# A kernel of two model blocks on one core: other buffers for the glu and w_out weights, silu and parts earlier in the order, and twelve row buffers for the expert gathers

## The chip, the cores and the metric

One core of a Trainium2 chip. The time is that of one execution on the device, in microseconds; lower is better. A kernel's time is the median of its runs.

## The reference, cut to what matters

A first block (attention, then a Fourier mixer, 256 tokens of width 2048) feeds a second one. All is float32. What the change touches lies in the second:

```python
yc = conformer_conv_group(...)        # conv, layer norm with gain and bias, then c * sigmoid(c)
z = gelu(y_ssm); ys = z * sigmoid(z @ glu_w)                    # 1024 x 1024
y = concat([rms_norm(yc, grp_norm_conv_g), rms_norm(ys, grp_norm_ssm_g)])
h = h + y @ w_out                                               # 2048 x 2048
h = h + mem_cross_attention(...)
hn = rms_norm(h, norm_ffn_g)
# peer: for each token and each of 8 heads
s1, i1 = top_k(q1 @ keys1, 16); s2, i2 = top_k(q2 @ keys2, 16)  # 128 keys a side
top_s, pos = top_k(s1[:, None] + s2[None, :], 16)               # of 256 sums
idx = i1 * 128 + i2 at pos;  g = softmax(top_s)
act = gelu(hn . u[idx]);  h += sum(g * act * v[idx])            # 128 rows of u and of v a token
```

## The kernel before, in words

Every engine has a program written out by hand in its own order: SP issues the weight loads, TensorE (pe_) multiplies, VectorE (v_) and ScalarE (a_) prepare operands and take results out, GpSimd (g_) issues the gathers. Programs wait on named moments; what stands behind a wait on the same engine waits with it.

**Memory.** The ring has eight units of 8 KB per partition, numbered 0 to 7. A load takes the next unit or units in a cycle over `c.units` of them, from `c.unit_next` (sp_slot, L262), and waits until the load that held them is used. In the split products units 6 and 7 hold the parts of the weights. The arena (30 K floats per partition) holds activations; views of it are placed by offset in K1 = 1024 floats.

**A split product.** Weights come as chunks of 128 x 512, `i` counting them over all blocks. ScalarE rounds a chunk to a high part (L398), VectorE subtracts to get the low part (L410), TensorE makes three products of parts (L489 to L492 by columns, L452 to L454 by rows). Four chunks of parts exist, so ScalarE's cast of chunk i waits until TensorE is done with chunk i - 4. `split` (L513) sets the order on ScalarE and VectorE: the part of chunk i, then what stands in `at` for chunk j = i - 3 (the number is j within its block; the function gets the block), then the block's `out`, then an aside step; after a job's last chunk its `end`. Jobs follow each other without a break: the first chunks of the next job are made ahead of the last work of the one before.

**Mixer.** sp_mixer (L2288) loads w_in, tables for the state part (unit 5), phases 0 to 7 of the state part (units 4 and 3 in turn), then glu's weights (two blocks of 8 chunks, four loads of one unit, cycling over units 0 to 2) and w_out's (four blocks of 16 chunks, eight loads of two units over units 0 to 5). TensorE runs the convolution, the column sums for the conv's layer norm, glu by columns, then w_out by rows with two sums for each block: one over the conv half and one over the state half, as each half has its own norm, applied behind the product (`add`). On ScalarE, glu's `end` runs conv_silu (L2648: all eight silus, from `cen` to `convT`), and w_out's first chunks run high(0) to high(3) (L2656, the high parts of y with the norm's gain, four columns each; 0 and 1 are the conv half) and the squares for the two norms. On VectorE glu's `end` is `gated` (L2558, z times sigmoid), and low(0) to low(3) (L2562) make the low parts of y in w_out's first block. TensorE's chunk k needs the low part of the chunk and of y's group k // 4. The norms' row sums (pe_row_sums, L2407) come behind chunks 3 and 11 of the first block.

**Experts.** TensorE makes the queries: head 0 alone, head 1 alone, then two heads at a time (pe_queries, L3026), from eight weight loads of one unit in units 0 to 5. Behind head 0, head 1 and the pair 2, 3 come their key scores (pe_choose). v_choose (L3109) picks the indices: copies the scores to `sc`, top 16 of each side, `cand`, top 16 of those, `eq` to look the indices up. It runs for head 0 and for head 1 at once (L3185 to L3188: copy of the query, choice), and later in ten steps between scored rows. g_experts (L3284) waits for the last weight load and gathers 512 times 128 rows of 2048 floats, one for each of the 128 partitions, in a fixed order: 36 of u, then v and u in turn. Gather n uses buffer n modulo ten: the eight units of the ring and two of the arena, those that hold no query weights first, then the six others in the order in which TensorE uses their weights up. VectorE scores u rows (L3219) and adds most v rows (L3207), TensorE adds three of eight v rows (L3071).

## Time and profile before

| | us |
|---|---|
| median of 3 runs | 3579.13 (3578.89 to 3579.28) |
| the profiled execution, its own time | 3582.07 |
| its span | 3580.6 |

Busy shares of the span: TensorE 74%, VectorE 74%, GpSimd 43%, ScalarE 29%. Mean rate of the DMA engines: 272 GB/s. Mean granted TensorE clock: 0.87 (1 is 2.4 GHz). The page gives shares over the whole span; a change to one stage has to be read in that stage, from the rows further down. All times in rows are from the start of the span.

### The profile page before, as it was taken

To read this page: it belongs to the slowest core of one execution; us is meant where nothing else is said; L and a number is where in the kernel's file an instruction comes from. 1 tells how busy PE (TensorE), PEld (TensorE's weight loads), DVE (VectorE), ACT (ScalarE), POOL (GpSimd) and SP (SyncE) were. 2 spreads that over 40 slices of the span, in tenths; PEclk is the share of its full clock that TensorE was granted. 3 is DMA by queue.
4 is the path that set the end of the run, shared out by engine and by line. 5 is a ranking of instruction groups with operands and counts; after the bars stand their busy time and mean duration, and the time that the engine had idled before them with its cause. 6 is when DMAs were issued, how large, how long until landed. Compare 5 with 4: busy or idle time off the path is not lost.

```text
span 3580.6 us, 35597 instructions
## 1 busy us (share of the span) xinstructions
PE 2650.4 (74%) x13300; PEld 2047.9 (57%) x13300; DVE 2657.4 (74%) x3789; ACT 1055.2 (29%) x1961; POOL 1554.6 (43%) x1943
## 2 busy tenths in 40 slices
PE   7989999987999999799988999614444444434445
PEld 6867897555999987699676897501111111111112
DVE  8977887767566655578855555798889798888775
ACT  2255253233444444354665535000000000000000
POOL 7887777750000000000000000387877776876663
PEclk9999999998999999999998999856676676776668
DMA  9876766634376645443204544799999999999998
GB/s 371 324 257 228 244 231 218 222 131 175 106 257 231 230 143 186 178 163 130 83 26 175 188 142 159 278 415 420 422 422 422 422 422 422 405 422 421 422 421 349
DMA packets 277965, 974.07 MB, mean 272 GB/s; under 512 B 14497, under 2 KB 30497, under 8 KB 208929
## 3 DMA queue, kind: packets, MB, share of 16 engines
q0 software_dynamic: 76592, 551.58, 37.2%
q1 hardware_dynamic: 198848, 411.70, 32.9%
q10 hardware_dynamic: 2352, 8.52, 0.6%
q8 instruction: 104, 1.70, 0.2%
q14 instruction: 69, 0.56, 0.0%
HBM read 957.07 MB, written 14.68 MB: 271 GB/s over the span
## 4 chain that ended last, share of the span: by engine, by line
PE 54%; DMA 19%; DVE 14%; POOL 6%; ACT 3%; issue 3%; ACTq 0%; SPq 0%; DVEq 0%; POOLq 0%
DMA ring<-in_peer_v,arena 9%; PE lin L489 7%; PE lin L491 6%; PE lin L492 6%; DMA ring<-in_peer_u,arena 5%; PE lin L452 5%; PE lin L454 5%; PE lin L453 5%; PE lin L3071 5%; POOL ring L3302 5%; PE lin L356 3%; PE lin L2374 3%; DMA arena<-in_peer_v,arena 2%; DVE mod_sums L811 2%; DVE weight_parts L410 2%
## 5 line engine op out<-in xcount | busy, mean ns | idle before, releaser
L410 DVE TENSOR_TENSOR weight_parts<-ring,weight_parts 128x512 fp32r<-128x512 f32 (+2 forms) x1010 | 687.7, 693 | 497.8 <-ACT weight_parts L398 492.1
L3071 PE MATMUL lin<-ring,diag 128*128 128x512 f32 x632 | 436.0, 854 | 619.8 <-DMA ring<-in_peer_v,arena 471.4
L398 ACT CAST weight_parts<-ring 128x512 fp32r<-128x512 f32 (+2 forms) x1010 | 610.9, 611 | 796.7 <-PE lin L492 386.5
L3071 PEld LDWEIGHTS lin<-ring,diag 128*128 128x128 f32 x632 | 168.9, 281 | 882.8 <-issue 809.9
L489 PE MATMUL lin<-parts,weight_parts 128*128 128x256 f32 x1984 | 571.0, 288 | 10.4 <-DVE weight_parts L410 10.4
L491 PE MATMUL lin<-parts,weight_parts 128*128 128x256 f32 x1984 | 564.3, 284 | 0.0
L492 PE MATMUL lin<-parts,weight_parts 128*128 128x256 f32 x1984 | 564.1, 284 | 0.0
L3219 DVE CUSTOM_DVE_ANT_0 ring<-ring,arena 128x2048 f32<-128x2048 f32 x204 | 465.5, 2290 | 128.8 <-DMA ring<-in_peer_u,arena 121.9
L2772 POOL DMA_DIRECT2D arena<-mem_keys x1 | 0.6, 575 | 1240.5 <-DVE weight_parts L410 1240.5
L3302 POOL DMA_INDIRECT ring<-in_peer_u,arena x204 | 373.7, 1832 | 338.0 <-DVE arena L3120 226.5
L452 PE MATMUL lin<-weight_parts,parts 128*128 128x512 f32 (+2 forms) x1124 | 435.2, 387 | 45.5 <-DVE weight_parts L410 21.8
L3302 POOL DMA_INDIRECT ring<-in_peer_v,arena x206 | 370.6, 1799 | 184.6 <-PE lin L3071 125.5
L453 PE MATMUL lin<-weight_parts,parts 128*128 128x512 f32 (+2 forms) x1124 | 426.3, 379 | 0.0
L454 PE MATMUL lin<-weight_parts,parts 128*128 128x512 f32 (+2 forms) x1124 | 426.3, 379 | 0.0
L489 PEld LDWEIGHTS lin<-parts,weight_parts 128*128 128x128 f32 x1984 | 383.5, 193 | 16.4 <-DVE weight_parts L410 12.4
L491 PEld LDWEIGHTS lin<-parts,weight_parts 128*128 128x128 f32 x1984 | 383.8, 193 | 0.4
L492 PEld LDWEIGHTS lin<-parts,weight_parts 128*128 128x128 f32 x1984 | 383.5, 193 | 0.0
L3207 DVE SCALAR_TENSOR_TENSOR arena<-ring,arena 128x2048 f32<-128x2048 f32 x127 | 298.5, 2350 | 40.0 <-DMA ring<-in_peer_v,arena 38.1
L452 PEld LDWEIGHTS lin<-weight_parts,parts 128*128 128x128 f32 x1124 | 213.7, 190 | 100.9 <-DVE weight_parts L410 33.4
L454 PEld LDWEIGHTS lin<-weight_parts,parts 128*128 128x128 f32 x1124 | 213.6, 190 | 39.3
L453 PEld LDWEIGHTS lin<-weight_parts,parts 128*128 128x128 f32 x1124 | 214.0, 190 | 37.4 <-issue 1.0
L811 DVE SCALAR_TENSOR_TENSOR mod_sums<-ring,silu_c,mod_sums 128x512 f32<-128x512 f32 x240 | 187.5, 781 | 5.2 <-DMA ring<-in_ada_w 0.8
(298 smaller groups left out, 3780.6 us busy)
## 6 DMA issues: line engine op xcount, KB each, us to landing
ring<-in_ada_w SPq DMA_DIRECT2D x96, 1024.0 KB, 8.3
ring<-in_w_in_fourier SPq DMA_DIRECT2D x64, 1024.0 KB, 8.2
ring<-in_w_kv_mem SPq DMA_DIRECT2D x32, 1024.0 KB, 7.6
ring<-in_w_in_attn SPq DMA_DIRECT2D x32, 1024.0 KB, 5.3
ring<-in_w_out_fourier SPq DMA_DIRECT2D x16, 2048.0 KB, 8.0
ring<-in_w_in SPq DMA_DIRECT2D x24, 1024.0 KB, 5.1
ring<-in_w_out_attn SPq DMA_DIRECT2D x8, 2048.0 KB, 8.6
ring<-in_w_out SPq DMA_DIRECT2D x8, 2048.0 KB, 8.2
```

The costliest lines, as they stand in the source:

```text
L398: c.nc.scalar.copy(c.w_parts[:, q, 0, 0:w], c.slot(load, L.kc, w)[:, k % L.kc, :]).then_inc(c.a_high.after(("high", L.name, i)), 1)
L410: c.nc.vector.tensor_tensor(c.w_parts[:, q, 1, 0:w], c.slot(load, L.kc, w)[:, k % L.kc, :], c.w_parts[:, q, 0, 0:w].bitcast(F32), ALU.subt ...
L452: c.nc.tensor.matmul(banks[t][:, 0:w], lhs(0, k, t), hi, start=(k % part == 0), stop=False)
L453: c.nc.tensor.matmul(banks[t][:, 0:w], lhs(0, k, t), lo, start=False, stop=False)
L454: mm = c.nc.tensor.matmul(banks[t][:, 0:w], lhs(1, k, t), hi, start=False, stop=(k % part == part - 1))
L489: c.nc.tensor.matmul(o, hi[:, b], rhs(0, k), start=(k == 0 and j % 2 == 0), stop=False, skip_group_check=True)
L491: c.nc.tensor.matmul(o, hi[:, b], rhs(1, k), start=False, stop=False, skip_group_check=True)
L492: mm = c.nc.tensor.matmul(o, lo[:, b], rhs(0, k), start=False, stop=(k == L.K - 1), skip_group_check=True)
L3071: mm = nc.tensor.matmul(X.sums[t][b][:, :], c.diag[:, X.diag_of(t, k), :], X.buf_of[t, 1, k][:, b * 512:(b + 1) * 512], start=(k == PE_ROW ...
L3207: nc.vector.scalar_tensor_tensor(out=X.H[:, t, :], in0=X.buf_of[t, 1, k], scalar=X.act[:, t, k:k + 1], in1=X.H[:, t, :], op0=ALU.mult, op1 ...
L3219: c.nc.vector.tensor_tensor_reduce(out=buf, in0=buf, in1=X.hn[:, t, :], scale=1.0, scalar=0.0, op0=ALU.mult, op1=ALU.add, accum_out=X.act[ ...
L3302: c.nc.gpsimd.indirect_dma_start(X.bufs[q], None, X.tables[table], bass.IndirectOffsetOnAxis(ap=X.idx[:, t, k:k + 1], axis=0)).then_inc(go ...
```

## The change

In sp_mixer glu's loads cycle over units 0 to 3, and w_out's begin at unit 4. The silus run in pairs behind chunks 3 to 6 of glu's second block, and the conv half's high and low parts behind its chunk 7, ahead of the sigmoid of that block and of `gated`. For that y's low parts are placed elsewhere (6 K1 and 19 K1). The other high and low parts and the squares for the conv norm shift by a few chunks, and the row sums of the conv norm go from chunk 3 to chunk 5. In the experts `sc`, `cand` and `eq` hold one group of heads instead of all, and two row buffers of 8 KB take the place that is left (17 and 19 K1). Head 1's query is copied by ScalarE, behind its part of the turned activations.

```diff
@@ -2261,7 +2261,13 @@
         self.stat = c.at(29 * K1, 4, SEQ)
         self.token = c.st[:, 42:54].rearrange("p (a b t) -> p a b t", a=2, b=3)
         self.L = Lin("w_out_mix", c.I["w_out_2"][0], 0, D)
-        self.R = Residual(c, self.L, "y_mix", c.at(9 * K1, KD * SEQ), c.at_r(25 * K1, KD * SEQ), c.at_r(17 * K1, KD * SEQ))
+        self.y = c.at(9 * K1, KD * SEQ)
+        self.y_hi = c.at_r(25 * K1, KD * SEQ)
+        self.y_lo = [c.at_r(6 * K1, NC * SEQ), c.at_r(19 * K1, NC * SEQ)]
+
+    def y_cols(self, a, k, t):
+        part = self.y_hi[:, k * SEQ:(k + 1) * SEQ] if a == 0 else self.y_lo[k // NC][:, k % NC * SEQ:(k % NC + 1) * SEQ]
+        return part[:, t * P:(t + 1) * P]
 
     def lo_part(self, q):
         return self.lo[q // 2][:, q % 2 * 1024:(q % 2 + 1) * 1024]
@@ -2300,8 +2306,9 @@
         yield from sp_load(c, (L.name, b, ch), L.src(b, w, ch), L.kc, w, units=1)
     for k in range(2, NC):
         yield from sp_phases(c, k)
+    c.units, c.unit_next = 4, 0
     yield from sp_weights(c, X.glu_lin)
-    c.units, c.unit_next = 2 * RING - 2, 0
+    c.units, c.unit_next = 2 * RING - 2, 4
     yield from sp_weights(c, X.L)
 
 
@@ -2400,8 +2407,8 @@
 
     yield from pe_split_cols(c, X.glu_lin, "z", X.z_cols, at={3: conv_variance})
     first = lambda f: lambda b: nothing() if b else f
-    yield from pe_split_rows(c, X.L, (X.R.name,), X.R.lhs, sums=2,
-                             at={3: first(pe_row_sums(c, "conv_rms", X.tmp)), 11: first(pe_row_sums(c, "ssm_rms", X.tmp2))})
+    yield from pe_split_rows(c, X.L, ("y_mix",), X.y_cols, sums=2,
+                             at={5: first(pe_row_sums(c, "conv_rms", X.tmp)), 11: first(pe_row_sums(c, "ssm_rms", X.tmp2))})
 
 
 def pe_row_sums(c, name, x):
@@ -2561,13 +2568,18 @@
 
     def low(q):
 
-        R, (_, g) = X.R, GROUP_NORMS[q // 2]
-        yield from v.wait_ge(("high", R.name, q))
+        g = GROUP_NORMS[q // 2][1]
+        yield from v.wait_ge(("high", "y_mix", q))
         for k in range(4 * q, 4 * q + 4):
-            s = slice(k * SEQ, (k + 1) * SEQ)
-            nc.vector.scalar_tensor_tensor(out=R.lo[:, s], in0=R.yT[:, s], scalar=c.col(g, k % NC), in1=R.hi[:, s].bitcast(F32),
-                                           op0=ALU.mult, op1=ALU.subtract).then_inc(
-                c.v_low.after(*([("low", R.name, q)] if k % 4 == 3 else [])), 1)
+            s, r = slice(k * SEQ, (k + 1) * SEQ), slice(k % NC * SEQ, (k % NC + 1) * SEQ)
+            nc.vector.scalar_tensor_tensor(out=X.y_lo[k // NC][:, r], in0=X.y[:, s], scalar=c.col(g, k % NC),
+                                           in1=X.y_hi[:, s].bitcast(F32), op0=ALU.mult, op1=ALU.subtract).then_inc(
+                c.v_low.after(*([("low", "y_mix", q)] if k % 4 == 3 else [])), 1)
+
+    def conv_low(b):
+        if b == 1:
+            yield from low(0)
+            yield from low(1)
 
     def add(b, half):
         n, w = X.L.blocks[b]
@@ -2585,9 +2597,8 @@
 
     first = lambda f: lambda b: nothing() if b else f()
     yield from v_jobs(c, [
-        Job(X.glu_lin, nothing, z_part, end=gated),
-        Job(X.L, lambda b: add(b, 1), at={0: first(lambda: low(0)), 2: first(lambda: low(1)), 5: first(lambda: low(2)),
-                                          7: first(lambda: low(3)), 9: lambda b: add(b, 0)})])
+        Job(X.glu_lin, nothing, z_part, at={NC - 1: conv_low}, end=gated),
+        Job(X.L, lambda b: add(b, 1), at={1: first(lambda: low(2)), 3: first(lambda: low(3)), 9: lambda b: add(b, 0)})])
 
 
 def v_column_rstd(c, X, name):
@@ -2645,21 +2656,24 @@
     def glu_out(b):
         yield from a_cols_act(c, X.glu_lin, lambda j: X.zs[:, j:j + 2, :], ACT.Sigmoid)(b)
 
-    def conv_silu():
-        yield from a.aside(0)
+    def conv_silu(k0):
         yield from a.wait_ge("conv_normed")
-        for k in range(NC):
+        for k in (k0, k0 + 1):
             nc.scalar.activation(X.convT[:, k, :], X.cen[:, k, :], ACT.Silu, bias=c.col("conv_ln_b", k),
                                  scale=c.col("conv_ln_g", k)).then_inc(
                 step.after(*(["conv_silu"] if k == NC - 1 else [])), 1)
 
     def high(q):
-        R, (_, g) = X.R, GROUP_NORMS[q // 2]
+        g = GROUP_NORMS[q // 2][1]
         yield from a.wait_ge("conv_silu" if q < 2 else "gated")
         for k in range(4 * q, 4 * q + 4):
             s = slice(k * SEQ, (k + 1) * SEQ)
-            nc.scalar.activation(R.hi[:, s], R.yT[:, s], ACT.Copy, scale=c.col(g, k % NC)).then_inc(
-                c.a_high.after(*([("high", R.name, q)] if k % 4 == 3 else [])), 1)
+            nc.scalar.activation(X.y_hi[:, s], X.y[:, s], ACT.Copy, scale=c.col(g, k % NC)).then_inc(
+                c.a_high.after(*([("high", "y_mix", q)] if k % 4 == 3 else [])), 1)
+
+    def conv_high():
+        yield from high(0)
+        yield from high(1)
 
     def squared(name, x, tmp, ready):
         yield from a.wait_ge(ready, ("full", ("sum", "conv_ln")))
@@ -2670,14 +2684,17 @@
         yield from a_rstd(c, name, (X.token[:, half, 1, :], X.token[:, half, 2, :]))
 
     first = lambda f: lambda b: nothing() if b else f()
+    second = lambda f: lambda b: f() if b == 1 else nothing()
     a.side, a.rate, a.owed = [a_conv_norm(c, X)], 0.5, 0
     yield from a_jobs(c, [
-        Job(X.glu_lin, glu_out, z_part, end=conv_silu),
+        Job(X.glu_lin, glu_out, z_part, at={
+            3: second(lambda: conv_silu(0)), 4: second(lambda: conv_silu(2)), 5: second(lambda: conv_silu(4)),
+            6: second(lambda: conv_silu(6)), 7: second(conv_high)}),
         Job(X.L, a_block_squares(c, X.L, X.H), at={
-            0: first(lambda: high(0)), 1: first(lambda: high(1)),
-            2: first(lambda: squared("conv_rms", X.convT, X.tmp, "conv_silu")), 4: first(lambda: high(2)), 6: first(lambda: high(3)),
+            0: first(lambda: high(2)), 2: first(lambda: high(3)),
+            3: first(lambda: squared("conv_rms", X.convT, X.tmp, "conv_silu")),
             7: first(lambda: squared("ssm_rms", X.ysT, X.tmp2, "gated")), 9: first(lambda: roots(0)), 15: first(lambda: roots(1))})])
-    c.moments[(X.R.name, "squares")] = (c.a_step.sem, c.a_step.value)
+    c.moments[("y_mix", "squares")] = (c.a_step.sem, c.a_step.value)
 
 
 def a_conv_norm(c, X):
@@ -2914,9 +2931,9 @@
         self.f_row = c.at(10 * K1, D)
         self.qT = c.at(12 * K1, E_HEADS, SEQ)
         self.keys = c.at(14 * K1, E_HEADS, E_KEYS)
-        self.sc = c.at(15 * K1, E_HEADS * 2, E_KEYS)
-        self.cand = c.at(17 * K1, E_HEADS, TOPK, TOPK)
-        self.eq = c.at(19 * K1, E_HEADS, TOPK, TOPK)
+        self.sc = c.at(15 * K1, HH * 2, E_KEYS)
+        self.cand = c.at(15 * K1 + 512, HH, TOPK, TOPK)
+        self.eq = c.at(16 * K1, HH, TOPK, TOPK)
         small = c.at(21 * K1, 16, 256)
         self.v1 = small[:, 0, :]
         self.i1 = small[:, 1, :].bitcast(U32)
@@ -2933,7 +2950,7 @@
         self.act = c.at(25 * K1 + 256, NT, E_SLOTS)
         self.idx = c.at(25 * K1 + 512, NT, E_SLOTS).bitcast(U32)
         self.bufs = [c.ring[:, i // 2, (i % 2) * D:(i % 2 + 1) * D] for i in range(2 * RING)] + [
-            c.at(26 * K1, D), c.at(28 * K1, D)]
+            c.at(17 * K1, D), c.at(19 * K1, D), c.at(26 * K1, D), c.at(28 * K1, D)]
         self.buf_of = {}
         self.tables = (c.I["peer_u_2"][0], c.I["peer_v_2"][0])
         self.sums, self.added, self.diag_holder = {}, None, {}
@@ -3117,18 +3134,18 @@
     for sd in range(2):
         key = ("key_scores", t, h0, sd)
         yield from v.wait_ge(("full", key))
-        nc.vector.tensor_copy(sc[:, hs, sd, :], c.bank[key][:, 0:n * E_KEYS].rearrange("p (a b) -> p a b", a=n)).then_inc(
+        nc.vector.tensor_copy(sc[:, 0:n, sd, :], c.bank[key][:, 0:n * E_KEYS].rearrange("p (a b) -> p a b", a=n)).then_inc(
             step.after(("free", key)), 1)
     yield True
     i1q, v1q = (x.rearrange("p (q k) -> p q k", k=TOPK) for x in (X.i1, X.v1))
-    yield from v_top16(c, lambda q: X.sc[:, 2 * h0 + q, :], lambda q: v1q[:, 2 * h0 + q, :],
+    yield from v_top16(c, lambda q: X.sc[:, q, :], lambda q: v1q[:, 2 * h0 + q, :],
                        lambda q: i1q[:, 2 * h0 + q, :], 2 * n)
     v1, i1f = halves(X.v1), halves(X.i1f)
     nc.vector.tensor_copy(X.i1f[:, ls], X.i1[:, ls]).then_inc(step.after(), 1)
-    vt(X.cand[:, hs], v1[:, hs, 0, :].unsqueeze(3).broadcast_to([P, n, TOPK, TOPK]),
+    vt(X.cand[:, 0:n], v1[:, hs, 0, :].unsqueeze(3).broadcast_to([P, n, TOPK, TOPK]),
        v1[:, hs, 1, :].unsqueeze(2).broadcast_to([P, n, TOPK, TOPK]), ALU.add).then_inc(step.after(), 1)
     tv, pv = by_head(X.top), by_head(X.pos)
-    yield from v_top16(c, lambda q: X.cand[:, h0 + q, :, :].rearrange("p a b -> p (a b)"),
+    yield from v_top16(c, lambda q: X.cand[:, q, :, :].rearrange("p a b -> p (a b)"),
                        lambda q: tv[:, h0 + q, :], lambda q: pv[:, h0 + q, :], n)
     vs(X.pi[:, ks], X.pos[:, ks], 4, None, ALU.logical_shift_right).then_inc(step.after(), 1)
     vs(X.pj[:, ks], X.pos[:, ks], 15, None, ALU.bitwise_and).then_inc(step.after(), 1)
@@ -3138,14 +3155,14 @@
     yield from v.wait_ge(step)
     iota = c.iota[:, :].unsqueeze(1).broadcast_to([P, TOPK, TOPK])
     for f, sd, e in ((X.pif, 0, X.e1), (X.pjf, 1, X.e2)):
-        for h in range(h0, h0 + n):
-            vt(X.eq[:, h], by_head(f)[:, h, :].unsqueeze(2).broadcast_to([P, TOPK, TOPK]), iota, ALU.is_equal).then_inc(
+        for h in range(n):
+            vt(X.eq[:, h], by_head(f)[:, h0 + h, :].unsqueeze(2).broadcast_to([P, TOPK, TOPK]), iota, ALU.is_equal).then_inc(
                 step.after(), 1)
         yield from v.wait_ge(step)
-        vt(X.eq[:, hs], X.eq[:, hs], i1f[:, hs, sd, :].unsqueeze(2).broadcast_to([P, n, TOPK, TOPK]), ALU.mult).then_inc(
+        vt(X.eq[:, 0:n], X.eq[:, 0:n], i1f[:, hs, sd, :].unsqueeze(2).broadcast_to([P, n, TOPK, TOPK]), ALU.mult).then_inc(
             step.after(), 1)
         yield from v.wait_ge(step)
-        nc.vector.tensor_reduce(by_head(e)[:, hs, :], X.eq[:, hs], AX_X, ALU.add).then_inc(step.after(), 1)
+        nc.vector.tensor_reduce(by_head(e)[:, hs, :], X.eq[:, 0:n], AX_X, ALU.add).then_inc(step.after(), 1)
         yield from v.wait_ge(step)
         yield True
     nc.vector.scalar_tensor_tensor(out=X.idxf[:, ks], in0=X.e1[:, ks], scalar=float(E_KEYS), in1=X.e2[:, ks],
@@ -3183,7 +3200,8 @@
         names = [("used", "ffn_g")] if t == NT - 1 else []
         vt(X.hn[:, t, :], X.hn[:, t, :], g_row, ALU.mult).then_inc(step.after(*names), 1)
     for h in range(HH):
-        yield from v_copy_out(c, ("query", h), X.qT[:, h, :], lambda: c.bank[("query", h)][:, 0:SEQ])
+        if h == 0:
+            yield from v_copy_out(c, ("query", h), X.qT[:, h, :], lambda: c.bank[("query", h)][:, 0:SEQ])
         v.side = [v_choose(c, X, 0, h, 1)]
         yield from v.aside(0)
     for n, (t, table, k) in enumerate(ORDER):
@@ -3245,6 +3263,8 @@
     yield from a_rms_rows(c, "ffn_x", lambda t: X.H[:, t, :], lambda t: X.hn[:, t, :])
     for q in range(KD // 4):
         yield from a_turn_out(c, ("ffn_x", q), lambda k: X.cols(4 * q + k), 4, NT, gain=lambda k: c.col("ffn_g", 4 * q + k))
+    for h in range(1, HH):
+        yield from a_copy_out(c, ("query", h), X.qT[:, h, :], lambda: c.bank[("query", h)][:, 0:SEQ])
     for h in range(HH):
         yield from a_choose(c, X, 0, h, 1)
     for h in range(HH, E_HEADS, HH):
```

## Rows read from the trace of the kernel before

**Rows 1.** The page's slices: rate of the DMA engines in each of 40 equal slices.

```profile
GB/s 371 324 257 228 244 231 218 222 131 175 106 257 231 230 143 186 178 163 130 83 26 175 188 142 159 278 415 420 422 422 422 422 422 422 405 422 421 422 421 349
```

**Rows 2.** Chain of waits, 1835 to 1975: start us, us, what.

```profile
1874.93 9.35 DMA ring<-in_w_out
...
1888.26 4.04 ACT arena L2652 x8
...
1892.80 1.61 ACT parts L2661 x4
1894.44 1.68 DVE parts L2568 x4
...
1903.81 4.76 PE aux L2414 x32
...
1921.79 3.47 PE aux L2414 x32
```

**Rows 3.** Timeline of ScalarE (ACT): start us, us, engine, line, op, tiles, count, idle before.

```profile
1872.07 0.62 ACT L398 CAST weight_parts<-ring 128x512 fp32r<-128x512 f32 x1 [0.82 <-PE lin L492]
...
1885.87 1.07 ACT L2160 ACTIVATE arena<-lin 128x512 f32<-128x512 f32 x2
1886.96 1.28 ACT L2652 ACT_TABLE_LOAD   x1
...
1913.62 0.62 ACT L398 CAST weight_parts<-ring 128x512 fp32r<-128x512 f32 x1 [1.58 <-PE lin L454]
```

**Rows 4.** Timeline of VectorE (DVE), same stretch.

```profile
1847.01 1.23 DVE L426 TENSOR_TENSOR parts<-arena,parts 128x1024 fp32r<-128x1024 f32 x1 [20.01 <-ACT parts L420]
...
1887.07 2.29 DVE L2560 TENSOR_TENSOR arena<-arena 128x2048 f32<-128x2048 f32 x1 [0.22 <-ACT arena L2160]
```

**Rows 5.** TensorE's timeline, then windows: busy times by engine, granted clock, DMA share, GB/s.

```profile
1896.25 0.77 PE L452 MATMUL lin<-weight_parts,parts 128*128 128x512 f32 x1 [17.02 <-DVE parts L2568]
...
1882.00:1883.50 1.50, 0.00 (x0) 0.00 (x0) 0.00 (x0) 0.00 (x0) 0.00 (x0) 0.63 1.06 392
...
1907.50:1912.00 4.50, 4.50 (x15) 3.73 (x15) 0.00 (x0) 0.57 (x1) 0.00 (x0) 0.50 1.04 381
```

**Rows 6.** Timelines at the queries: TensorE three rows, ScalarE one.

```profile
2252.48 0.80 PE L3021 MATMUL aux<-arena 64*128 64x128 f32 x4 [4.64 <-DVE arena L368]
2253.21 16.35 PE L3037 MATMUL lin<-arena,ring 128*128 128x256 f32 x64
...
2270.89 27.89 PE L3037 MATMUL lin<-arena,ring 128*128 128x256 f32 x128
...
2269.60 0.58 ACT L373 COPY arena<-lin 128x512 f32<-128x512 f32 x1 [5.67 <-PE lin L3037]
```

**Rows 7.** Timelines at the first gathers: last weight load (SP), GpSimd (POOL), all gathers' landing.

```profile
2247.88 0.37 SPq L280 DMA_DIRECT2D ring<-in_peer_w_q  x1
...
2253.97 1.02 POOL L3302 DMA_INDIRECT ring<-in_peer_u,arena  x1 [226.47 <-DVE arena L3120]
...
2299.06 1.83 POOL L3302 DMA_INDIRECT ring<-in_peer_u,arena  x1 [5.97 <-PE lin L3037]
...
DMA to landing us min/median/max: 5.6/18.7/22.2
```

**Rows 8.** Windows in the experts, columns as in rows 5.

```profile
2251.00:2257.00 6.00, 4.52 (x13) 3.58 (x14) 4.53 (x26) 0.21 (x1) 2.43 (x3) 0.50 0.44 128
2400.00:2420.00 20.00, 5.37 (x8) 2.03 (x8) 20.00 (x27) 1.48 (x2) 18.17 (x7) 0.79 0.95 383
2820.00:2840.00 20.00, 9.84 (x12) 4.03 (x13) 14.01 (x11) 0.81 (x3) 13.34 (x9) 0.59 1.02 424
3040.00:3060.00 20.00, 10.30 (x16) 3.70 (x15) 18.90 (x26) 1.69 (x2) 18.48 (x6) 0.84 0.95 381
3060.00:3080.00 20.00, 6.64 (x9) 2.63 (x9) 19.58 (x37) 0.00 (x0) 15.93 (x12) 0.59 0.97 385
```

**Rows 9.** Timeline of VectorE, the tenth gathered row.

```profile
2307.32 2.29 DVE L3219 CUSTOM_DVE_ANT_0 ring<-ring,arena 128x2048 f32<-128x2048 f32 x1 [6.45 <-DMA ring<-in_peer_u,arena]
```

## The prediction, made before the changed kernel was run

> **What bounds the kernel now.** I read four views in this order. The slices first [rows 1]: from the 27th on the DMA engines move 415 to 422 GB/s (one slice 405) until the last, of 349, so that stretch (the experts) is bound by the bytes of its 512 row gathers of 1.049 MB each, 2.485 us apiece at 422 GB/s. Before it the rate is mostly a half to a third of that, and the chain of waits runs mostly through TensorE. Only four places of the kernel can be worth anything to this change: the hand-over from the gate product (glu) to w_out, the hand-over from the queries to the gathers, and two dents in the saturated stretch.
>
> Hand-over to w_out: in the chain of waits [rows 2] TensorE's glu work ends at 1879.2, the first w_out load is issued at 1874.93 and lands 9.35 us later, and then eight silus, four high parts and four low parts follow one another before TensorE starts at 1896.25 after 17.02 us idle [rows 5]. Its granted clock was down at 0.50 (1.2 GHz) when it started, and again in 1907.5 to 1912 [rows 5].
>
> Hand-over to the gathers: TensorE is idle for 4.64 us until 2252.48, after head 1's query, waiting for VectorE's copy of it, which stands behind head 0's whole choice [rows 6]. Six of the ten row buffers hold query weights, so GpSimd issues four gathers from 2253.97 on and then one each time TensorE is done with a weight chunk (six of them, 4 to 8 us apart); the tenth goes out at 2299.06 [rows 7]. Only from there are the DMA engines full.
>
> **Part 1, glu and w_out in units of their own.** Today glu cycles through three units and w_out's first load (two units) needs one that glu's last chunk holds. With the change glu's last load takes unit 3 and w_out's first units 4 and 5, held by tables and phases that VectorE's state work has read by 1827 (it is idle for 20.01 us before 1847.01 [rows 4]). Both loads then land before 1845. That removes the wait for the DMA. On SP nothing is moved ahead of anything late: the other w_out loads follow in the same order, the second when glu's first two chunks are used (about 1863), and it is not needed before 1900.
>
> **Part 2, silu and parts inside glu's second block.** I lay out ScalarE from the casts of [rows 3]; silu's input is ready before that. Cast 14 ends at 1872.7. Table load 1.28 and two silus of 0.505: 1875.0. Cast 15 (0.6) ends at 1875.6; TensorE needs its low part at 1877.8, so glu isn't delayed: slack 1.5. Then silu pair, cast 16, silu pair, cast 17, silu pair, cast 18: 3 x (1.0 + 0.6) gives 1880.4. Two high groups of 1.7: 1883.8. The sigmoid of block 1, which stood right behind the casts, now waits for all this and needs its table again: 1.28 + 1.07, done 1886.2. VectorE: the first low group ends at 1883.8, the second at 1885.5, the gating product of 2.29 [rows 4] at 1888.5.
> So TensorE starts w_out at 1883.9 instead of 1896.25, 12.3 earlier. What is late next: w_out's fourth chunk, whose low part stands behind the gating product on VectorE: ready 1889.2. ScalarE's high(2) waits for the gating product too, and casts 20 and up are queued behind it, TensorE behind them: cast 20 at 1890.8, low parts of chunks 4 and 5 at 1891.5 and (behind low(2), 1.67) 1893.8. Chunk 5 ends at 1895.3. The sums of the conv norm, moved from behind chunk 3 to behind chunk 5, wait for a square of 1.9 that ends at 1895.5, and take 3.5 to 4.8 (4.76 for them here, 3.47 for the other norm's [rows 2]): done 1899.1 to 1900.4. The old kernel has chunk 5 and the same sums done at 1913.6 (the cast released then [rows 3]). From there both do the same work at the same pace. Gain 13.2 to 14.5; I take **13.5**. Bounds: 14.5 with the clock at 2.4 GHz in the sums; 11 if half clock lasts 4.4 us into chunks 6 and 7 as it did around 1907 to 1912, which costs 2.2. TensorE's gap shrinks from 17 to 4.7 us, but the clock fell about 3.2 us after the matmuls stopped (granted 0.63 in 1882 to 1883.5 [rows 5]), so I let it fall.
> The change makes ScalarE switch tables once more. In [rows 3] the Silu switch takes 1.28 and the first silu begins 0.02 behind it; two such switches stand in my chain. ("ScalarE: Activation LUTs" of the Trainium skill, What ACT_TABLE_LOAD costs, puts every switch at 1283 ns and a drain of about 1380 ns. The trace has the 1.28 and nothing of a drain. By the page, as an estimate, both switches together cost 2.8 more, and the gain would be about 11.)
> Memory stage: TensorE-bound, its loads follow TensorE; all of it only moves earlier. Profile rows below are given in the old kernel's times.
>
> **Part 3, head 1's query copied by ScalarE.** ScalarE is idle there; a copy of twice the size takes 0.58 [rows 6]. TensorE has the scores' input at 2248.4 and starts the next query group at 2249.1 instead of 2253.21: 4.1. The gap of 4.64 also cost clock (granted 0.50 from 2251 to 2257 [rows 8]): that group took 16.35 us and the next ones 13.9 each [rows 6]. With a gap of 0.7 there is no fall: 2.5 more. Sum **6.6**. The last chunk is then used at 2292.4. VectorE loses a copy of 0.42. GpSimd's first gather doesn't move: it waits for the last weight load, issued at 2247.88 when head 1's matmuls are done, 6.1 before that gather [rows 7].
>
> **Part 4, two more buffers.** Six gathers go out before the first wait, not four, and twelve have gone when the last chunk is used. DMA has idle time for them there. **2 x 2.485 = 4.97.** VectorE gains as much: it has scored rows 1 to 9 when row 10 lands at 2307.3, after 6.45 idle [rows 9]; now it is row 12 that lands at 2300.7, with two rows (4.6) and a choice step (1.1) less left, 12.3 in all against the DMA's 11.6.
> The dents: 383 GB/s in 2400 to 2420, 381 and 385 in 3040 to 3080 [rows 8] against 422, that is 1.85 + 1.94 + 1.75 = **5.5** us, where the buffers were all with VectorE (busy 20.0, 18.9 and 19.6 of 20). Two more rows of slack are 4.97 in each, more than either dent, so I take all back. The scratch shared by the groups costs nothing: all its users are VectorE, in the same order, and each step already waits for the last. A third buffer-related wait: a group's indices are ready by its 15th scored row, the gather that needs them is issued at the 20th or later.
>
> **Sum**: 13.5 + 6.6 + 5.0 + 5.5 = 30.6. Against the profiled execution's own 3582.07 that is 3551.5; the three runs have a median of 3579.13, 2.9 lower, so I forecast **3548.5**. Its own range is 3543 to 3553: 14.5 in the mixer on one side, with 4 for waits that fall differently; 11 and half the dents on the other.
>
> **Rivals.**
> A, chance 0.17: the dents stay (VectorE's backlog, not the number of buffers, sets them) and the query group stays slow: 13.5 + 4.1 + 5.0 = 22.6, **3556.5**. For it: VectorE is busy 20.0 of 20 in the first [rows 8]. Against: in dents of under 2 us two rows are enough.
> B, 0.09: in w_out the clock and the queue on ScalarE take back more, so that only 9 is left there: **3553**.
> C, 0.04: nothing of parts 3 and 4 reaches the end, as VectorE becomes the bound from 2300 on: 13.5, **3565.6**. Against it: further on VectorE is busy only 14.0 of 20 [rows 8].
> D, 0.03: SP's w_out load still comes late because a unit isn't free; parts 1 and 2 then give 10.5 (cast at 1884.3, start at 1885.8): **3551.5**.
> E, 0.02: deeper queue, higher rate. "DMA: Bandwidth & Descriptors" (Trainium skill, Specifications) has a fabric ceiling of 435 GB/s, which would be 3% more; as an estimate 38 us, 3511. In rows alone: 422 is moved with ten in flight, and the highest window of 20 us has 424 [rows 8], 0.5% or 6 us more, **3542**.
> F, slower, 0.03: twelve gathers in flight on one queue, two of them into memory beside the scratch that VectorE uses in each choice, lower the rate of all gathers in the 1250 us from 2300 on. Each per cent costs 12.5, so 2.5% (411 GB/s) eats the gain and 3.2% makes **3588**. For it: a gather lands up to 22.2 us after its issue as it is [rows 7], a queue already deep. Against: from the 28th slice to the last but one all but one keep 420 to 422 [rows 1], whatever the engines do.
> G, 0.02: both hand-overs give back three quarters, under 7.2 is left: **3573**.
>
> **Numbers.** 0.2% is 7.2 us, about what a measurement of this kernel can tell from no change. Faster: forecast 0.60 and A to E, 0.95; same 0.02 (G); slower 0.03 (F). The range for eight in ten, 3543 to 3560, takes in forecast, A, B and D, and the joint low bounds 11 + 8.9.
>
> **What the next profile would show.** Right: w_out's first load issued by 1830; TensorE idle under 6 us before its first w_out matmul, near 1884; head 1's copy on ScalarE, the gap before the second scores under 1 us and the query group at 13.9; six gathers before GpSimd's first wait on TensorE; slices of 421 to 423 with no dent. Wrong: glu matmuls waiting for cast 15 or 16; TensorE idle over 3 us at chunks 3 to 5; a gather rate under 418; VectorE idle for landings gone but DMA share under 1.

## The result, and the profile after

The changed kernel takes 3560.18 us (median of 6 runs, 3556.59 to 3567.35), beside 3579.2 for the kernel before in 6 runs on the same chip: a ratio of 0.9946, 95% interval 0.9936 to 0.9957, 19 us or 0.54% less. The two were run again beside the last experiments: 3557.76 (5 runs) against 3581.89 (9 runs), 0.9937, 0.9923 to 0.9951. Forecast were 3548.5, range 3543 to 3560: right in sign, 11.7 us too low, and at the very edge of the range (by the medians 0.2 us above it, by the ratio, 0.9946 x 3579.13 = 3559.8, 0.2 inside).

**How stages are compared.** The program of the first 1840 us is the same in all kernels, yet glu's first product stands anywhere between 1843.66 and 1855.62 us in the fourteen profiled executions. What follows repeats far better, so I measure from event to event in each profiled execution: glu's first product, w_out's first product, the memory stage's first transpose on TensorE, the experts' first transpose, and VectorE's addition of the last gathered row. The two profiled executions of the changed kernel differ by 0.02, 0.02, 0.00 and 0.16 us in these. Across kernels that have the same program in a stretch the scatter is larger: the four with the old mixer give 47.30 to 47.59 and 152.56 to 152.89 us up to w_out and to the memory stage, but 224.54 to 226.24 from there to the experts; the four with the old experts (before, mixer part, units, silu and parts) give 1339.23 to 1339.95. One execution's difference under 0.7 us (1.6 in the memory stage) therefore shows nothing by itself; that the new mixer costs the memory stage 1.4 us rests on five executions of 227.52 to 227.62. The last column has the median of the runs; units, silu and parts, copy, buffers and ten buffers ran once each.

| us | glu to w_out | glu to memory | memory to experts | experts to last row | time |
|---|---|---|---|---|---|
| before | 47.36 | 152.65 | 226.10 | 1339.72 | 3579.2 |
| after | 34.67 | 141.01 | 227.52 | 1327.07 | 3560.2 |
| after, once more | 34.69 | 141.03 | 227.52 | 1327.23 | 3557.8 |
| mixer part alone | 34.68 | 140.98 | 227.60 | 1339.63 | 3567.6 |
| experts part alone | 47.45 | 152.71 | 226.11 | 1327.07 | 3567.2 |
| units alone | 40.28 | 145.56 | 226.85 | 1339.23 | 3570.1 |
| silu and parts alone | 43.94 | 151.88 | 227.03 | 1339.95 | 3579.1 |
| copy alone | 47.30 | 152.56 | 224.54 | 1333.73 | 3571.9 |
| buffers alone | 47.59 | 152.89 | 226.24 | 1334.33 | 3578.3 |
| after with ten buffers | 34.68 | 141.03 | 227.60 | 1333.12 | 3565.7 |
| sums spread | 34.69 | 137.04 | 226.41 | 1328.91 | 3554.0 |
| order of reuse | 34.68 | 141.04 | 227.62 | 1318.15 | 3551.9 |
| both | 34.69 | 137.02 | 226.40 | 1319.01 | 3548.4 |
| both, first gather sooner | 34.69 | 137.02 | 226.40 | 1317.02 | 3546.2 |

By the stages the change is worth 11.64 - 1.42 + 12.65 = **22.9 us** (0.64%). That lies at the edge of the first interval and inside the second, and the 7.7 us between it and the forecast sum of 30.6 is what has to be explained. The rest of the 11.7, 4.0 us, lies in no stage that was compared: runs of one kernel lie up to 11 us apart, and the two profiled executions differ by 23.5, of which 0.62 ahead of glu.

**The hand-over to w_out.** ScalarE's timeline in the changed kernel (start us, us, engine, line, operation, tiles, count, idle before); it answers to [rows 3]:

```profile
1871.43 0.62 ACT L398 CAST weight_parts<-ring 128x512 fp32r<-128x512 f32 x1 [0.82 <-PE lin L492]
1872.07 1.28 ACT L2662 ACT_TABLE_LOAD   x1
1873.37 1.09 ACT L2662 ACTIVATE arena<-arena,colpack_sb 128x256 f32<-128x256 f32 x2
1874.37 0.60 ACT L398 CAST weight_parts<-ring 128x512 fp32r<-128x512 f32 x1
...
1879.39 3.30 ACT L2671 ACTIVATE parts<-arena,colpack_sb 128x256 fp32r<-128x256 f32 x8
1882.70 1.28 ACT L2160 ACT_TABLE_LOAD   x1
1884.00 1.09 ACT L2160 ACTIVATE arena<-lin 128x512 f32<-128x512 f32 x2
...
1887.54 1.71 ACT L2671 ACTIVATE parts<-arena,colpack_sb 128x256 fp32r<-128x256 f32 x4 [1.95 <-DVE arena L2567]
```

The silus stand between the casts and hold up nothing, the high parts follow, then the sigmoid of glu's second block. Start of w_out, from TensorE's timeline, answering to [rows 5]; then, from the chain of waits, the two blocks of row sums that answer to the L2414 rows of [rows 2]:

```profile
1882.94 0.76 PE L452 MATMUL lin<-weight_parts,parts 128*128 128x512 f32 x1 [4.35 <-DVE parts L2575]
```

```profile
1894.38 3.63 PE aux L2421 x32
...
1907.92 3.46 PE aux L2421 x32
```

TensorE starts 12.69 us sooner after glu's first product, with 4.35 idle instead of 17.02. The conv norm's sums end at 1898.0. Now windows of the same profile (us, busy time by engine, granted clock, DMA share, GB/s):

```profile
1898.00:1899.00 1.00, 1.00 (x6) 0.81 (x6) 0.00 (x0) 0.00 (x0) 0.00 (x0) 0.92 0.91 344
1899.00:1902.00 3.00, 3.00 (x9) 2.33 (x8) 0.69 (x1) 2.01 (x2) 0.00 (x0) 0.50 1.05 404
1902.00:1907.00 5.00, 5.00 (x23) 4.12 (x22) 2.27 (x8) 4.07 (x7) 0.00 (x0) 0.97 0.19 66
1913.00:1916.00 3.00, 3.00 (x9) 2.32 (x8) 0.69 (x1) 0.91 (x2) 0.00 (x0) 0.52 1.05 409
1988.00:2001.00 13.00, 9.50 (x43) 9.13 (x44) 9.12 (x17) 9.16 (x16) 0.00 (x0) 0.50 0.02 7
```

TensorE is busy throughout, yet its granted clock halves (0.50, that is 1.2 GHz) right behind each of the two blocks of sums, and again in the memory stage's first products. There the kernel before has 0.74 in the same 13 us, counted from 1.3 us ahead of the first transpose:

```profile
2000.30:2013.30 13.00, 9.54 (x55) 9.17 (x56) 9.72 (x18) 9.51 (x17) 0.00 (x0) 0.74 0.02 7
```

**The hand-over to the gathers.** TensorE, answering to [rows 6]:

```profile
2237.47 0.49 PE L3038 MATMUL aux<-arena 64*128 64x128 f32 x4 [0.46 <-ACT arena L373]
2237.89 14.08 PE L3054 MATMUL lin<-arena,ring 128*128 128x256 f32 x64
...
2253.30 27.89 PE L3054 MATMUL lin<-arena,ring 128*128 128x256 f32 x128
```

The gap of 4.64 us is 0.46, and the query group takes 14.08 instead of 16.35. GpSimd's timeline, the first, eighth, ninth and twelfth gather, answering to [rows 7]; and the time from issue to landing over all gathers:

```profile
2244.11 1.02 POOL L3322 DMA_INDIRECT ring<-in_peer_u,arena  x1 [227.46 <-DVE arena L3115]
...
2252.92 2.58 POOL L3322 DMA_INDIRECT ring<-in_peer_u,arena  x1 [0.31 <-issue]
2260.74 2.84 POOL L3322 DMA_INDIRECT ring<-in_peer_u,arena  x1 [5.24 <-PE lin L3054]
...
2281.46 3.04 POOL L3322 DMA_INDIRECT ring<-in_peer_u,arena  x1 [4.74 <-PE lin L3054]
```

```profile
DMA to landing us min/median/max: 5.8/23.8/28.0
```

Eight gathers go out before the first wait on TensorE, where I forecast six. Then the stretch in which the DMA engines are full: the page's slices, answering to [rows 1], and windows, answering to [rows 8]:

```profile
GB/s 370 310 269 227 249 230 224 228 116 178 123 231 244 239 152 169 186 150 159 43 79 163 190 143 160 312 422 422 422 422 422 422 421 422 421 422 421 422 421 331
```

```profile
2400.00:2420.00 20.00, 8.53 (x13) 3.03 (x12) 19.62 (x28) 0.00 (x0) 14.69 (x11) 0.73 1.01 421
...
3040.00:3060.00 20.00, 9.36 (x13) 3.93 (x14) 19.52 (x38) 0.00 (x0) 15.10 (x11) 0.69 1.01 419
3060.00:3080.00 20.00, 6.84 (x12) 2.46 (x10) 19.57 (x21) 2.68 (x6) 16.69 (x9) 0.83 1.01 422
```

No dent is left: 419 to 422 where 381 to 385 stood. But the last slice is lower than before, 331 against 349. I took the dents for 5.5 us of gain. That slice is the first sign that they aren't.

### The profile page after: what moved, and what is told of

Same layout as the page of the kernel before. It is cut to its first block, busy times and chain, and to the rows that moved or that the text cites. A ratio compares the mean times of both kernels' runs of the same rounds, so it can differ in the third digit from the quotient of the medians.

```text
span 3557.1 us, 35597 instructions
## 1 busy us (share of the span) xinstructions
PE 2662.4 (75%) x13300; PEld 2054.8 (58%) x13300; DVE 2654.5 (75%) x3788; ACT 1057.9 (30%) x1963; POOL 1553.6 (44%) x1943
## 4 chain that ended last, share of the span: by engine, by line
PE 53%; DMA 18%; DVE 14%; POOL 8%; issue 4%; ACT 3%; ACTq 0%; SPq 0%; DVEq 0%; POOLq 0%
PE lin L489 7%; PE lin L491 6%; PE lin L492 6%; DMA ring<-in_peer_u,arena 6%; PE lin L452 5%; PE lin L454 5%; PE lin L453 5%; DMA ring<-in_peer_v,arena 5%; POOL ring L3322 5%; DMA arena<-in_peer_v,arena 4%; PE lin L2381 3%; PE lin L3088 3%; PE lin L356 3%; POOL arena L3322 3%; DMA arena<-in_peer_u,arena 2%
## 5 line engine op out<-in xcount | busy, mean ns | idle before, releaser
L3088 PE MATMUL lin<-ring,diag 128*128 128x512 f32 x512 | 354.6, 857 | 428.3 <-DMA ring<-in_peer_v,arena 366.7
L489 PE MATMUL lin<-parts,weight_parts 128*128 128x256 f32 x1984 | 571.5, 288 | 10.5 <-DVE weight_parts L410 10.4
L3088 PEld LDWEIGHTS lin<-ring,diag 128*128 128x128 f32 x512 | 138.0, 283 | 643.1 <-issue 576.3
L3237 DVE CUSTOM_DVE_ANT_0 ring<-ring,arena 128x2048 f32<-128x2048 f32 x170 | 387.6, 2288 | 105.8 <-DMA ring<-in_peer_u,arena 99.9
L3322 POOL DMA_INDIRECT ring<-in_peer_u,arena x170 | 297.6, 1751 | 306.9 <-DVE arena L3115 227.5
L3088 PE MATMUL lin<-arena,diag 128*128 128x512 f32 x256 | 186.0, 894 | 291.7 <-DMA arena<-in_peer_v,arena 196.1
L3322 POOL DMA_INDIRECT ring<-in_peer_v,arena x170 | 314.8, 1852 | 151.9 <-PE lin L3088 102.9
L3088 PEld LDWEIGHTS lin<-arena,diag 128*128 128x128 f32 x256 | 71.6, 294 | 403.8 <-issue 382.1
L3225 DVE SCALAR_TENSOR_TENSOR arena<-ring,arena 128x2048 f32<-128x2048 f32 x106 | 249.0, 2349 | 33.1 <-DMA ring<-in_peer_v,arena 31.7
L452 PEld LDWEIGHTS lin<-weight_parts,parts 128*128 128x128 f32 x1124 | 213.8, 190 | 83.4 <-DVE weight_parts L410 30.8
L454 PEld LDWEIGHTS lin<-weight_parts,parts 128*128 128x128 f32 x1124 | 213.8, 190 | 39.6
```

The lines of the kernel that those rows point to most:

```text
L452: c.nc.tensor.matmul(banks[t][:, 0:w], lhs(0, k, t), hi, start=(k % part == 0), stop=False)
L454: mm = c.nc.tensor.matmul(banks[t][:, 0:w], lhs(1, k, t), hi, start=False, stop=(k % part == part - 1))
L489: c.nc.tensor.matmul(o, hi[:, b], rhs(0, k), start=(k == 0 and j % 2 == 0), stop=False, skip_group_check=True)
L3088: mm = nc.tensor.matmul(X.sums[t][b][:, :], c.diag[:, X.diag_of(t, k), :], X.buf_of[t, 1, k][:, b * 512:(b + 1) * 512], start=(k == PE_ROW ...
L3225: nc.vector.scalar_tensor_tensor(out=X.H[:, t, :], in0=X.buf_of[t, 1, k], scalar=X.act[:, t, k:k + 1], in1=X.H[:, t, :], op0=ALU.mult, op1 ...
L3237: c.nc.vector.tensor_tensor_reduce(out=buf, in0=buf, in1=X.hn[:, t, :], scale=1.0, scalar=0.0, op0=ALU.mult, op1=ALU.add, accum_out=X.act[ ...
```

## The experiments

Six kernels take the change apart, a seventh leaves only the two buffers out, two change one thing that the traces pointed to, two join these, and the last is the changed kernel once more.

**Halves.** The mixer part alone (all of sp_mixer's, low, high and silu's edits), and the experts part alone (scratch, buffers, copy).

> Only the mixer's half of the change (units, silu and parts earlier, sums behind chunk 5), the experts as before. I measure in the trace from glu's first matmul to the memory stage's first transpose (152.65 us before, 141.01 in the changed kernel) and from the experts' first transpose to the last gathered row's addition (1339.72 and 1327.07). Theory of two separate gains: the first stretch 140.5 to 143, the second within 1.5 of 1339.7; time 11 to 12 us under before, ratio 0.9965 to 0.9972. Rival, the gain of the mixer only moves a wait in the experts (part of the 12.65 there is owed to the earlier start): the second stretch 1330 to 1336.

> Only the experts' half (scratch for one group, twelve buffers, head 1's query copied by ScalarE), the mixer as before. Separate gains: first stretch 152 to 154, second 1326 to 1328.5, time 12 to 13 us under before, ratio 0.9962 to 0.9968. Rival as above: second stretch 1331 or more.

Measured: 3567.61 us, ratio 0.9961 (0.9946 to 0.9976), and 3567.22 us, 0.9958 (0.9941 to 0.9974). By stages the mixer part gives 11.67 and loses 1.50 in the memory stage, 10.2 in all; the experts part gives 12.65. Their sum is 22.8, and the change gave 22.9. They add, so each can be looked into by itself. All four stretches lie where the theory of separate gains had them; both ratios are 0.0004 below the ranges expected.

**The mixer taken apart.** First the units alone, with silus and parts where they were:

```diff
+    c.units, c.unit_next = 4, 0
     yield from sp_weights(c, X.glu_lin)
-    c.units, c.unit_next = 2 * RING - 2, 0
+    c.units, c.unit_next = 2 * RING - 2, 4
```

> Before, with only the ring units of glu and w_out changed. The DMA wait goes, the chain of silus, high and low parts behind glu's last sigmoid stays: casts 16 to 18 at about 1878, silus to 1885.5, first low part 1889.5. Theory that the two parts of the mixer overlap: from glu's first matmul to w_out's first 40.5 to 42 us (47.36 before, 34.67 with both). Rival, the load was the whole wait: 36 to 38.

Then the reverse: all the rest of the mixer part, with the two unit lines as before.

> The changed order of silu and parts with the old ring units: w_out's first load goes out when glu's last chunk is used. By the same theory the silus wait behind the cast that waits for this load (they stand between casts 15 and 18 on ScalarE), so the load is followed by three silu pairs, casts and two high parts again: 44 to 47 us, hardly better than before. Rival, from my forecast (its rival D): start right behind the landing, 36.5 to 38.

Timelines of SP and ScalarE, units alone:

```profile
1818.56 51.77 SPq L280 DMA_DIRECT2D ring<-in_w_out  x3
```

```profile
1873.58 1.31 ACT L2160 ACTIVATE arena<-lin 128x512 f32<-128x512 f32 x2
1874.91 1.28 ACT L2653 ACT_TABLE_LOAD   x1
1876.20 4.04 ACT L2653 ACTIVATE arena<-arena,colpack_sb 128x256 f32<-128x256 f32 x8
```

and ScalarE, silu and parts alone:

```profile
1872.12 1.09 ACT L2661 ACTIVATE arena<-arena,colpack_sb 128x256 f32<-128x256 f32 x2
1882.37 0.62 ACT L398 CAST weight_parts<-ring 128x512 fp32r<-128x512 f32 x1 [9.16 <-DMA ring<-in_w_out]
```

Units alone take 7.08 us off the way to w_out, the rest alone 3.42, both together 12.69, so 2.2 more than their sum. (From glu to w_out both are a little under the ranges expected, by 0.2 and 0.1 us, and far from the rivals' 36 to 38.) The second timeline shows why: behind the second pair of silus ScalarE waits 9.16 us for w_out's first weights, and the last two pairs and the high parts queue behind that cast. The load has to be early for the silus to move. Alone, their 3.42 has shrunk to 0.77 by the memory stage.

**The experts taken apart.** The copy by ScalarE alone, and the buffers (with the shared scratch) alone:

```diff
+    for h in range(1, HH):
+        yield from a_copy_out(c, ("query", h), X.qT[:, h, :], lambda: c.bank[("query", h)][:, 0:SEQ])
```

```diff
-            c.at(26 * K1, D), c.at(28 * K1, D)]
+            c.at(17 * K1, D), c.at(19 * K1, D), c.at(26 * K1, D), c.at(28 * K1, D)]
```

> Before, with only head 1's query copied by ScalarE. Theory: TensorE's wait of 4.64 us and the half clock behind it go, the tenth gather goes out 6.7 earlier, and everything behind is paced by the gathers: from the experts' first transpose to the last row's addition 1333.0 (6.7 less than 1339.7). Rival, VectorE (busy without a break from the tenth row on) is the bound: 1336 or more.

> Before, with only the scratch for one group and twelve buffers. Two gathers more before the flood give 5.0 by either theory. The dents: by my forecast they are lost time of all DMA engines and all 5.5 us come back, the stretch is 1329.2. Rival, formed from the changed kernel's end (there one sixteenth of the DMA rate goes on for 8 us after the rest has stopped): one DMA engine is behind the others and sets the pace, it keeps working through most of a dent, and only about 1 to 2 us come back: 1332.7 to 1333.7, and at the end the engines stop 8 to 10 us apart, not 5.

The copy is worth 5.99 us (0.7 less than expected); the buffers 5.39, not 10.5, and 0.6 less than the rival had at least. Together the halves of this part gave 12.65, so 1.3 more than their sum. Most of that isn't an effect of one on the other. With the buffers alone the experts' first transposes, whose program is that of the kernel before, happened to fall under the half clock (6.64 us instead of 5.08), and the last gather that waits for query weights, the twelfth, goes out 72.03 us behind the first transpose; in the kernel before it is the tenth, at 71.41. With the copy it is 64.62 to 64.92 in five executions. Rows of the kernel with the buffers alone:

```profile
2229.16 6.64 PE L590 MATMUL aux<-ident,arena 128*128 128x128 f32 x32 [4.09 <-DVE arena L727]
...
2301.19 1.70 POOL L3302 DMA_INDIRECT ring<-in_peer_u,arena  x1 [5.96 <-PE lin L3037]
```

So the copy moves this gather by 6.5 to 6.8 us. From it to the last row's addition it is 1267.36 to 1268.80 us in the six executions with ten buffers and the old order of reuse, and 1262.30 to 1262.61 in the five with twelve: 5.8 less on average. Two gathers are 4.97, which leaves about 0.9 for the dents. Windows of the kernel with the buffers alone, the second place of dents, then its last 16 us up to the last row's landing:

```profile
3020.00:3040.00 20.00, 9.65 (x13) 4.00 (x14) 19.96 (x31) 1.68 (x5) 16.27 (x6) 0.67 1.02 424
3040.00:3060.00 20.00, 8.24 (x12) 2.92 (x11) 18.82 (x24) 1.69 (x2) 17.56 (x9) 0.67 1.01 422
3060.00:3080.00 20.00, 9.48 (x13) 3.95 (x14) 19.52 (x38) 0.00 (x0) 13.10 (x10) 0.67 1.02 423
```

```profile
3547.49:3563.49 16.00, 12.64 (x21) 5.24 (x22) 8.10 (x5) 0.00 (x0) 0.00 (x0) 0.79 0.44 184
```

The dents are gone and the time has not come back; it is lost at the end. The same last 16 us in the kernel before and in the changed one, and windows of 4 us from the changed one's end:

```profile
3551.36:3567.36 16.00, 12.52 (x22) 5.11 (x23) 8.08 (x4) 0.00 (x0) 0.00 (x0) 0.79 0.71 297
```

```profile
3527.88:3543.88 16.00, 12.64 (x21) 5.19 (x22) 8.10 (x4) 0.00 (x0) 0.00 (x0) 0.79 0.47 197
...
3534.00:3538.00 4.00, 1.93 (x5) 0.67 (x4) 2.35 (x1) 0.00 (x0) 0.00 (x0) 0.91 0.27 115
3538.00:3542.00 4.00, 4.00 (x8) 1.73 (x7) 2.35 (x1) 0.00 (x0) 0.00 (x0) 0.67 0.06 27
```

A DMA share of 0.06 is one engine of sixteen, and 27 GB/s is a sixteenth of 422: in the last 6 us of the changed kernel one engine works off its part of the last gathers while fifteen have nothing left. The landing times of the sixteen parts of the last gather lie 9.5 us apart (5.2 before). One engine is a little slower than the others, and the gathers in flight let it fall behind: the spread grows to 9.5 us over 1250 us, 0.7%, so its pace is about 2.50 us a gather where the mean is 2.485. (Read from the 61st to the 281st gather, the last part lands every 2.503 us and the first every 2.485; it is one part alone that falls back, as all others of the last gather land within 2.2 us.) Where a dent stops the stream, the others wait and it catches up. Less was moved in those last 16 us by 16 x (297 - 197) / 422 = 3.8 us at full rate in the changed kernel, and 4.3 with the buffers alone.

**Buffers taken out again.** The changed kernel with ten buffers:

```diff
-            c.at(17 * K1, D), c.at(19 * K1, D), c.at(26 * K1, D), c.at(28 * K1, D)]
+            c.at(26 * K1, D), c.at(28 * K1, D)]
```

> The changed kernel with the two new row buffers taken out again, so ten as before; all else as changed. Theory (the buffers are worth two gathers, 5.0, and the dents next to nothing, 0.4): experts' stretch 1332.2 to 1332.8 (1327.1 with twelve). Rival: with the copy by ScalarE in place the dents are deeper, since VectorE's later choices meet a stream that started earlier, so the buffers hold back more than in the kernel with the buffers alone: 1333.7, as in the kernel with only the copy. Rival two: buffers and copy pay for the same idle time in the DMA engines, then under 1331.

The experts' stretch is 1333.12, 6.05 longer than with twelve: the buffers give 4.97 and 1.1. That is between the theory's 1332.8 and the rival's 1333.7, and closer to both than the scatter of 0.7 us lets one tell. (It also prices the copy beside the mixer part: 1339.63 with the mixer part alone, so 6.5, about the forecast's 6.6.) Its windows:

```profile
2400.00:2420.00 20.00, 6.77 (x9) 2.88 (x10) 19.52 (x39) 0.00 (x0) 16.61 (x12) 0.59 1.00 413
3020.00:3040.00 20.00, 10.61 (x16) 4.09 (x16) 18.87 (x33) 1.69 (x2) 18.06 (x7) 0.76 0.95 378
3040.00:3060.00 20.00, 6.34 (x8) 2.41 (x8) 19.52 (x35) 0.00 (x0) 16.34 (x11) 0.67 0.98 381
...
3534.86:3550.86 16.00, 12.31 (x22) 5.11 (x23) 8.07 (x4) 0.00 (x0) 0.00 (x0) 0.79 0.72 299
```

Dents of 0.4 + 2.1 + 1.9 = 4.4 us are back, and the last 16 us have 299 GB/s again, which is 3.9 us at full rate more than with twelve buffers: 4.4 - 3.9 = 0.5 should be left, and 1.1 is, a difference within the scatter. The landings show the catching up: the spread is 6.0 us ahead of the dents (at 3023) and 2.4 behind them (at 3086), and in the changed kernel 7.3 and 6.4 at the same places.

**The sums spread over four chunks.** To see whether the clock falls of w_out belong to the blocks of 32 products with one column each, I put eight of them behind each of four chunks:

```diff
-    yield from pe_split_rows(c, X.L, ("y_mix",), X.y_cols, sums=2,
-                             at={5: first(pe_row_sums(c, "conv_rms", X.tmp)), 11: first(pe_row_sums(c, "ssm_rms", X.tmp2))})
+    parts = {5: ("conv_rms", X.tmp), 11: ("ssm_rms", X.tmp2)}
+    yield from pe_split_rows(c, X.L, ("y_mix",), X.y_cols, sums=2, at={
+        k + i: first(pe_row_sums(c, name, x, i)) for k, (name, x) in parts.items() for i in range(4)})
```

> The changed kernel with each norm's row sums in four parts behind four chunks of w_out (5 to 8 and 11 to 14). In the changed kernel the granted clock falls to 0.50 twice, each time near the end of 3.5 us of products with one column, for 3.4 us. Theory: no stretch holds only such products any more, the falls go, and from glu's first matmul to the memory stage's first transpose it is 137.5 (141.0 now), the time 3 to 3.5 under the changed kernel. Rival, the falls come from somewhere else (the weight loads, the mean over a longer time): 140.5 to 141.5.

Measured: 3554.04 us, ratio 0.9916 (0.9899 to 0.9934). Windows of this kernel, and below those of the changed one:

```profile
1896.00:1906.00 10.00, 10.00 (x58) 8.65 (x57) 5.08 (x13) 6.29 (x8) 0.00 (x0) 1.00 0.61 212
1909.00:1919.00 10.00, 10.00 (x56) 8.66 (x57) 4.37 (x11) 4.01 (x10) 0.00 (x0) 1.00 0.62 210
```

```profile
1896.00:1906.00 10.00, 10.00 (x47) 8.41 (x48) 2.80 (x6) 5.15 (x7) 0.00 (x0) 0.83 0.61 210
1909.00:1919.00 10.00, 10.00 (x49) 8.44 (x49) 3.45 (x8) 2.06 (x4) 0.00 (x0) 0.83 0.61 210
```

The clock stays at full speed, with the same weight loads beside it (212 and 210 GB/s against 210 and 210), so the rival of the loads is out. glu to memory shrinks by 3.97 us: 3.4 for the two falls, and TensorE's only wait in w_out, 0.86 us at 1923.55 in the changed kernel, is gone too (the divided sums take a little longer than the block). The memory stage gets back 1.11 of the 1.42 that it had lost. The experts' stretch is 1.84 longer: its first 32 transposes now start under the half clock (5.99 us instead of 5.08), and the wait ahead of the key scores of the pair is 1.41 us instead of 0.68. By the stages that is 3.97 + 1.11 - 1.84 = 3.2 us.

**The order in which buffers are used again.** In the changed kernel gathers 9 to 12 wait for query weights, one every 7 us, while buffers whose rows VectorE has scored lie free (it is done with the first at 2254.7, and the ninth gather goes out at 2260.74). Here the free ones are taken again first:

```diff
+    early = len(order) - len(holder) + 2
-        q = order[n % len(order)]
+        q = order[n] if n < early else order[(n - early) % len(order)]
```

> The changed kernel with another order of buffers: the first eight gathers as now, but gathers 9 to 16 use the same eight buffers again, and the four that wait for TensorE's last weight chunks come in from the 17th on. The queries then hold nothing up. DMA engines had 11.6 us idle between the first gather and the flood (shares 0.79, 0.74 and 0.89 of 20 us). Theory (the gathers' start and one engine's pace of 2.50 us set the end): 10 to 11.5 less, the stretch 1316 to 1317 instead of 1327.1, time about 3549. Rival, VectorE's scoring with the first choice in it (some 100 us for the 36 first rows) becomes the bound and gives back what its own idle time of about 9.7 us there doesn't cover: 1319 to 1324.

Measured: 3551.92 us, ratio 0.9911 (0.9891 to 0.9930); the stretch is 8.92 us shorter, between the two. Windows of the changed kernel, and below those of this one:

```profile
2260.00:2280.00 20.00, 20.00 (x95) 17.60 (x94) 18.91 (x37) 0.59 (x1) 6.40 (x3) 1.00 0.74 284
2280.00:2300.00 20.00, 1.84 (x14) 1.24 (x12) 12.87 (x33) 0.58 (x1) 15.18 (x12) 0.61 0.89 356
```

```profile
2260.00:2280.00 20.00, 20.00 (x99) 17.55 (x99) 19.45 (x37) 0.59 (x1) 16.18 (x8) 1.00 1.01 425
2280.00:2300.00 20.00, 9.01 (x47) 7.55 (x45) 19.65 (x48) 0.59 (x1) 16.57 (x11) 0.82 1.01 420
...
3020.00:3040.00 20.00, 8.08 (x12) 3.23 (x13) 19.19 (x30) 0.00 (x0) 18.17 (x7) 0.67 0.95 380
```

The DMA engines are full from 2260 on. In return the stream now runs so far ahead that VectorE, 19 of 20 us busy, falls behind at 3020, and a dent of 2.0 us is back.

**Both, and the first gather sooner.** In the second of these kernels GpSimd's first gather doesn't wait for the last query weights to land (the loop that is left only sets the order in which the programs are written out):

```diff
-    yield from g.wait_ge(("used", last_load(c.memory.L)), ("used", ("parts", c.memory.L.name)),
-                         ("in", last_load(X.q_lins[-1])))
+    yield from g.wait_ge(("used", last_load(c.memory.L)), ("used", ("parts", c.memory.L.name)))
+    while ("in", last_load(X.q_lins[-1])) not in c.moments:
+        yield None
```

> Both repairs in one kernel: the row sums of the two norms in parts of eight products spread over four chunks, and the order in which row buffers are used again shortened so that a gather reuses one sooner after the first round. Alone each changed another stretch, so theory: they add. glu's first matmul to the memory stage's first transpose 137.0 (141.0 in the changed kernel), the experts' first transpose to the last gathered row's addition 1318 to 1320 (1327.1), together 11 to 13 us less than the changed kernel, 3547 to 3549. Rival: the gathers are bound from the experts' first transpose on, so that an earlier start shows in full, and there is no interplay at all either way; then the two spans are exactly those of the kernels with one repair (137.04 and 1318.15) to 0.2. Rival two: what the sums give back, the clock in the experts' first products takes again, as in the kernel with the sums alone (1328.9 against 1327.1): then 1320, and only 9.5 to 10.5 less.

> The kernel with both repairs, and GpSimd's first gather no longer waits for the landing of the last query weights; it goes when its indices are there, 3.9 us sooner in the changed kernel. Theory: the DMA engines have one gather and a half more moved when the stretch with full rate begins, if the weights' landing is not delayed by it: experts' stretch 2 to 3.5 us shorter than with both repairs alone. Rival: VectorE, 19.5 to 20 of 20 us busy from 2260 on, can't score rows sooner, so buffers come free no sooner and 0 to 1 us is left. Second rival: the rows are ahead of the last query weights in the queues, so head 1's matmuls or the pairs' come later, and the stretch is 1 to 3 us longer.

> The changed kernel once more, on the same chip and beside the same runs of the kernel before as those with the repairs. Stage spans as in its first profile to 0.2: glu to w_out 34.7, glu to memory 141.0, experts' stretch 1327.1. Ratio to before 0.9946 give or take 0.001.

Measured: both 3548.36 us, ratio 0.9906 (0.9891 to 0.9921); with the sooner gather 3546.15, 0.9904 (0.9888 to 0.9920). The stages of the two repairs add but for 0.9 us in the experts (1319.01 against 1318.15), about what the half clock costs the experts' first transposes (6.00 us here), so rival two holds in part. The sooner gather (2.95 us nearer to the experts' first transpose) takes 2.0 off the stretch, the low end of what the theory had; between these two kernels the runs can't tell, only the stages. The changed kernel beside them had 0.9937. So the best version found is 4.0 + 1.1 + 10.1 = 15.2 us under the changed kernel by its stages, and 11.6 by the medians.

## Why the forecast was right in sign and 7.7 us too high in gain

**The wait for the load: right.** w_out's first load is issued at 1822.90 (forecast by 1830) and the wait of 9.35 us [rows 2] is gone. So rival D is out, and its price was wrong too: with a late load, silu and parts gave 3.42 and not 10.5, since only two of the four pairs get ahead of the cast that waits for it.

**ScalarE's order laid out by hand: right to a microsecond.** Forecast were the high parts' end at 1883.8, the sigmoid's at 1886.2 and w_out's start at 1883.9, all in the old kernel's times; measured 1882.69, 1885.09 and 1882.94, in an execution that stood 0.62 earlier at glu. The conv norm's sums were forecast to end at 1899.1 to 1900.4 and end at 1898.0. With the 0.62 taken off that is 15.0 us sooner than the old kernel's 1913.6. So at that place the gain was above the forecast's 14.5, not below it.

On the table load the trace bears the forecast out and not the page: both loads take 1.28 us and what follows begins 0.02 behind each. "ScalarE: Activation LUTs" of the Trainium skill, What ACT_TABLE_LOAD costs, adds a drain of about 1380 ns to every switch. By it, as an estimate, w_out would have started 1.4 us later than it did.

**"From there both do the same work at the same pace": the step that failed in the mixer.** Behind that place, where chunk 5 and the sums are done, TensorE has two spells at half clock (3.4 us each by the trace, costing 1.7 each) that the old order doesn't have there, and the memory stage loses 1.42: 15.0 - 3.4 - 1.4 = 10.2 against 13.5. The old order did have one fall at its conv norm's sums ([rows 5], 0.50 from 1907.5 to 1912), but it was over at 1913.6, so the 15.0 already counts it. My low bound of 11 had one such spell, of 4.4 us in chunks 6 and 7, and I took the value near the other end; there were two, the second behind the other norm's sums, and the memory stage's loss came from outside what I had priced. Spreading the sums removed both falls, so without the undivided blocks of 32 products with one column there are none; but a block doesn't bring a fall by itself. The other norm's block had none behind it in the kernel before [rows 2, 3.47 us at 1921.79; granted clock 1.00 from 1925 to 1929] and none with the units alone (1.00 from 1913 to 1917), and why isn't shown. Of the 1.42 in the memory stage 1.1 went with the falls. The rest stays open.

**The copy: right.** 4.1 for the gap and 2.5 for the clock, 6.6: measured 6.0 alone and 6.5 beside the mixer part, and 6.5 to 6.8 at the last gather that waits for query weights.

**Two gathers: right.** The stretch behind the last such gather is 5.8 us shorter with twelve buffers, 4.97 and a bit. A detail was wrong and cost nothing: eight gathers, not six (it is six with the buffers alone), went ahead of the first wait, but the engines are full only from the twelfth, at 2281.46.

**The dents: the larger failure.** They disappeared exactly as forecast, but "I take all back", 5.5 us, brought about 1 (1.1 in one comparison, 0.9 on average). The step took the mean rate of sixteen engines for the pace of the last one. What the mean gained in the dents, fifteen engines spent idle at the end, 3.8 us of it. Rival A had 22.6 in all and the stages show 22.9, but by another mechanism on both sides: the dents didn't stay and the query group isn't slow.

**Sum by the stages:** mixer 10.2 of 13.5, copy 6.5 of 6.6, gathers 5.0 of 5.0, dents 1.1 of 5.5.

**The other rivals.** B comes nearest in the mixer, with 9 for the 10.2 measured, but the clock took back 3.4 there and the queue on ScalarE nothing that shows: the sums ended sooner than forecast. C and G fell with the 12.65 of the experts part. E and F both need another rate than 422 GB/s with twelve in flight, and the slices stand at 421 and 422. ("DMA: Bandwidth & Descriptors" of the Trainium skill, Specifications, has 435 GB/s as the fabric's ceiling; no window of 20 us that was read here has over 425.)

## What to carry to other kernels

Where a stream of transfers bounds the kernel, price what is gained in its middle by the slowest of the DMA engines, and read the last microseconds: a share of a sixteenth there means that one engine sets the end and that holes filled in earlier pay little. Lay out the engine that orders the hand-over by hand, instruction by instruction (it was good to a microsecond here), but carry the clock on beyond the hand-over: small products moved to another time can cost as much as a wait. When runs of one kernel lie 10 us apart and stages repeat to 0.7 us or better, compare stages, and look at the clock in a stage's first products before a difference of 1 us is given a cause.

## What the runs showed of the hardware

- With twelve gathers of 1.049 MB in flight one of the sixteen DMA engines falls up to 9.5 us behind over 1250 us (0.7% slower); with ten and two dents it ends 5.2 behind. Over all kernels the parts of the last gather land 3.2 to 7.5 us apart with ten buffers, and 9.2 to 10.7 with twelve where no dent was over 1.4 us (7.6 with the dent of 2.0 in the new order of reuse alone). In all four kernels whose end was read, the share near the end is 0.05 or 0.06, one engine of sixteen.
- TensorE's granted clock falls to 0.50 while TensorE is busy without a gap, behind 3.5 us of products with one column, in some places and not in others; broken into blocks of eight (0.95 to 1.05 us each) they leave it at 1.00.
- A stage's first products under the half clock cost it 0.9 us with the sums spread (5.99 against 5.08 for 32 transposes). Where the fall lies isn't set by the program alone: four kernels with the same program up to there took 5.08, 5.08, 5.35 and 6.64 us. That moves a later, untouched stage by 1 to 2 us in either direction.
